# Low halves of the weights formed by GpSimd in pieces of 256 columns, in an fp32r four-layer transformer kernel

## The reference

```python
def conv_glu_ffn(n, w_up, conv_w, conv_b, w_down):
    gate, up = jnp.split(n @ w_up, 2, axis=-1)
    gp = jnp.pad(gate, ((0, 0), (CONV_WIDTH - 1, 0), (0, 0)))
    conv = conv_b
    for j in range(CONV_WIDTH):
        conv = conv + gp[:, j:j + s] * conv_w[j]
    return (jax.nn.silu(conv) * up) @ w_down
```

## Time and profile before

| what | value |
|---|---|
| median of 3 runs | 2933.06 us (2922.97 to 2939.97) |
| the profiled execution, its own time | 2924.7 us |
| its span, first to last instruction | 2922.2 us |
| granted TensorE clock, mean over the span | 0.957 |
| TensorE matmul busy | 2723.0 us, 93% |
| DVE busy | 1739.8 us, 60% |
| ACT busy | 1095.2 us, 37% |
| GpSimd busy | 1027.7 us, 35% |
| DMA engines, mean busy share | 21.6% |

### The profile page before, as it was taken

One profiled execution on the slowest core, in us unless ns is written; L12 is line 12 of the kernel. 1 busy time (PEld: TensorE's weight loads), 2 busy tenths in 40 slices (PEclk: granted clock), 3 DMA queues, 4 the chain that ended last, 5 costly groups with the idle time before them and its releaser, 6 DMA issues.

```text
span 2922.2 us, 34757 instructions
## 1 busy us (share of the span) xinstructions
PE 2723.0 (93%) x11434; PEld 2003.5 (69%) x11434; DVE 1739.8 (60%) x2256; ACT 1095.2 (37%) x1682; POOL 1027.7 (35%) x385
## 2 busy tenths in 40 slices
PE   6999999999998999999698988999989898899997
PEld 5654788887764678888375455788757644587875
DVE  4655774586386577377559346827634944583672
ACT  2345332223144343232543545323344345532333
POOL 2220344443321234444144123544424411344452
PEclk9998899999998899999799999999999998999999
DMA  3110123232211123222111011222311110122221
GB/s 135 65 44 30 65 93 104 90 102 86 79 51 36 43 86 107 87 96 98 39 58 51 29 37 65 96 91 93 103 66 58 44 43 22 63 92 96 94 97 68
DMA packets 56071, 212.17 MB, mean 73 GB/s; under 512 B 6193, under 2 KB 6449, under 8 KB 55857
## 3 DMA queue, kind: packets, MB, share of 16 engines
q1 hardware_dynamic: 55120, 209.60, 21.6%
q10 hardware_dynamic: 864, 1.44, 0.2%
HBM read 208.92 MB, written 2.10 MB: 72 GB/s over the span
## 4 chain that ended last, share of the span: by engine, by line
PE 72%; DVE 11%; ACT 6%; issue 5%; POOL 3%; DVEq 1%; DMA 0%; ACTq 0%; POOLq 0%
PE bank_G L464 20%; PE bank_G L466 19%; PE bank_G L465 19%; PE bank_S L1093 4%; POOL wlo L411 3%; PE bank_O L1103 2%; DVE conv_up L724 2%; PE bank_X L1113 2%; PE bank_S L511 1%; DVE mx L1985 1%; ACT whi L437 1%; DVE prod L744 1%; PE bank_X L1658 1%; PE bank_X L793 1%; DVE scores_t L1636 1%
## 5 line engine op out<-in xcount | busy, mean ns | idle before, releaser
L411 POOL TENSOR_TENSOR wlo<-raw,whi 128x1024 fp32r<-128x1024 f32 (+1 forms) x363 | 984.8, 2714 | 1760.7 <-ACT whi L437 1760.6
L464 PE MATMUL bank_G<-n_hi,whi 128*128 128x512 f32 x2392 | 977.4, 409 | 62.6 <-DVE n_lo L568 30.1
L466 PE MATMUL bank_G<-n_hi,wlo 128*128 128x512 f32 x2392 | 945.0, 395 | 0.0
L465 PE MATMUL bank_G<-n_lo,whi 128*128 128x512 f32 x2392 | 944.3, 395 | 0.0
L464 PEld LDWEIGHTS bank_G<-n_hi,whi 128*128 128x128 f32 x2392 | 458.1, 192 | 206.0 <-issue 69.5
L437 ACT ACTIVATE whi<-raw 128x1024 fp32r<-128x1024 f32 (+1 forms) x363 | 403.4, 1111 | 369.4 <-PE bank_G L466 353.8
L466 PEld LDWEIGHTS bank_G<-n_hi,wlo 128*128 128x128 f32 x2392 | 456.6, 191 | 99.5
L465 PEld LDWEIGHTS bank_G<-n_lo,whi 128*128 128x128 f32 x2392 | 458.2, 192 | 95.9 <-issue 7.7
L634 DVE SCALAR_TENSOR_TENSOR h<-h,mixed 128x512 f32 (+1 forms) x96 | 70.1, 730 | 393.3 <-ACT mixed L443 393.3
L464 PE MATMUL bank_G<-a_hi,whi 128*128 128x512 f32 x704 | 275.3, 391 | 5.6 <-DVE a_lo L746 3.6
L465 PE MATMUL bank_G<-a_lo,whi 128*128 128x512 f32 x704 | 274.0, 389 | 0.0
(11 more groups left out here) (280 smaller groups left out, 2706.3 us busy)
## 6 DMA issues: line engine op xcount, KB each, us to landing
raw<-in_w_mix_in SPq DMA_DIRECT2D x42, 512.0 KB, 3.2
raw<-in_w_out SPq DMA_DIRECT2D x32, 512.0 KB, 3.3
raw<-in_w_hyb_in SPq DMA_DIRECT2D x25, 512.0 KB, 3.3
raw<-in_w_diff_in SPq DMA_DIRECT2D x24, 512.0 KB, 3.3
raw<-in_w_up0a SPq DMA_DIRECT2D x22, 512.0 KB, 3.2
raw<-in_w_up0b SPq DMA_DIRECT2D x22, 512.0 KB, 3.2
raw<-in_w_up1a SPq DMA_DIRECT2D x22, 512.0 KB, 3.3
raw<-in_w_up1b SPq DMA_DIRECT2D x22, 512.0 KB, 3.3
```

What stands on the lines that cost most here:

```text
L411: pool.tensor_tensor(b.wlo[:, g.slot, 0:width], b.raw[:, g.slot, 0:width], b.whi[:, g.slot, 0:width], ALU.subtract).then_inc(b.lo_ready, 1)
L464: pe.matmul(out, b.whi[:, g.slot, w], hi[:, k, :], start=(k == 0), stop=False)
L465: pe.matmul(out, b.whi[:, g.slot, w], lo[:, k, :], start=False, stop=False)
L466: mm = pe.matmul(out, b.wlo[:, g.slot, w], hi[:, k, :], start=False, stop=(k == pieces - 1))
```

## The change

The subtraction of a tile is issued as several instructions of 256 columns each instead of one over the full width: four for a tile of 1024 columns, and six for one of 1408 (five of 256 and one of 128). Only the last of them raises lo_ready; the two waits ahead of the first stay. The product of the scan in mixer_pool is left as it was. The arithmetic, the buffers and the order of all other instructions are the same.

```diff
@@ constants
 ROW = 4 * T
 ARENA = 21056
+LO_PIECE = 256
 PAD = 2
@@ split_lo
     pool.wait_ge(b.hi_ready, g.at(1))
     wait(pool, b.gemm_done, g.at(-1))
-    pool.tensor_tensor(b.wlo[:, g.slot, 0:width], b.raw[:, g.slot, 0:width], b.whi[:, g.slot, 0:width],
-                       ALU.subtract).then_inc(b.lo_ready, 1)
+    for first in range(0, width, LO_PIECE):
+        x = slice(first, min(first + LO_PIECE, width))
+        ins = pool.tensor_tensor(b.wlo[:, g.slot, x], b.raw[:, g.slot, x], b.whi[:, g.slot, x], ALU.subtract)
+    ins.then_inc(b.lo_ready, 1)
```

## The result

| | kernel before | changed kernel |
|---|---|---|
| median of the runs | 2928.68 us (2922.97 to 2939.97, 7 runs) | 2949.21 us (2945.81 to 2950.34, 7 runs) |
| ratio to before, 95% interval | | 1.0058 [1.0039, 1.0077] |
| profiled execution, own time | 2924.7 us | 2950.11 us |
| its span | 2922.2 us | 2948.1 us |
| granted clock, mean | 0.957 | 0.956 |

The change makes the kernel slower by 0.58%. Between the two profiled spans lie 25.9 us, where the prediction's sum said 26; between the two medians lie 20.5. Lines behind the edit stand three higher now (L411 is L414, L464 is L467, L724 is L727).

The account below looks back on a forecast made before the run. TensorE was busy 93% of the span, with DVE held up by GpSimd and low halves sometimes awaited. Terms 3 + 12 + 5 + 4 + 3 + 7 - 4 - 4 = +26 on 2924.7, plus 8.4 to the median: 2959 us, range 2930 to 2990.

Parts of the forecast that it names:

- Block 1: Feed-forward up pairs of block 1: low half up to 1.47 us later just fits slack 1.5; +3 us for jitter.
- the first down tiles: First tile of each down group: in block 1 1.26 us late, four times, +5 us; in block 2 +4.
- Block 2, first failing term: Up pairs of block 2: low half 0.52 us late, 0.25 lost now regained; net 0.27 over 44 pairs, +12 us.
- two tiles behind each other don't add up: Up pairs of block 2: two late tiles cost no double, since a late tile gives the next its time back.
- The loss of now: Up pairs of block 2: TensorE already loses 0.25 us a pair through DVE's chain; it goes, as prod comes sooner.
- few other starts: Third tiles of some groups: an estimated four starts wait for GpSimd, 0.39 to 0.84 us each, +3 us.
- The mixers: Mixers of block 2: some four starts in each wait for a later low half, half absorbed; 8 x 0.9, +7 us.
- DVE hogs the port: Rival: dense DVE taps in 18 mixer turns keep GpSimd out at piece boundaries; +36 to +72 us on top, chance 0.09.
- The norms and the attention: Gains from DVE held up less: -4 us at three norm places, -4 us in attention.
- DVE freed: Rival: fewer DVE instructions slip in, block 2's slack of 0.77 us holds; -26 us, 2907 us, chance 0.14.
- The pieces flow without a gap: Rival: DVE is not let in between pieces and is held longer; +24 us, within the 0.55 for late low halves.
- No difference: Rival for the whole kernel: both effects stay below 10 us or cancel; 2933 us, chance 0.22.

Follow-up runs that it names:

- e9: e6 with DVE waiting for the up tile's low half ahead of its third tap; 2947.17 us, ratio 1.0055 to the kernel before.
- e5: Kernel before with only the gate tiles of block 2's up groups in pieces of 256 columns; 2941.78 us, ratio 1.0051.
- e11: The changed kernel with one DVE wait for a low half in each mixer of block 2; 2936.13 us, ratio 1.0028 to the kernel before.
- the last version: e10 with one DVE wait for a low half in each mixer of block 2; 2899.89 us, ratio 0.9897 to the kernel before.
- e10: Kernel before with piece sizes chosen per group (256, 512 or whole), first down tiles of block 2 whole; 2907.52 us, ratio 0.9926.
- e4: The changed kernel with pieces of 128 columns everywhere instead of 256; 3023.16 us, ratio 1.0324 to the kernel before.
- e6: Kernel before with only the up tiles of block 2's up groups in pieces of 256 columns; 2952.94 us, ratio 1.0082.
- e3: The changed kernel with pieces of 512 columns everywhere instead of 256; 2919.09 us, ratio 0.9962 to the kernel before.

## Why the prediction was right, and where its terms were not

The forecast was 2959 us, within 2930 to 2990, slower. The median is 2949. The 10 us between are nearly all the offset: I added 8.4 us to the profiled execution, because the three runs shown had a median of 2933.06, and seven runs have one of 2928.68; the changed kernel's median lies 0.9 below its own profiled execution.

**The prices held.** 0.13 us a piece and 0.45 for each DVE instruction let in, both taken from whole low halves, measure 0.14 (256 columns at 2.16 ns are 0.55, the spacing with DVE idle is 0.69 to 0.70 in some 580 boundaries) and 0.45 (1.14 to 1.15 in some 330 more; e9 shows the same by taking it away). TensorE's 0.13 us behind a low half, which the prediction took from a row that it did not show, is the same in every pair of the changed kernel (1843.75 to 1843.88). The row, of the kernel before:

```profile
1803.28 2.83 POOL L411 TENSOR_TENSOR wlo<-raw,whi 128x1024 fp32r<-128x1024 f32 x1 [3.62 <-ACT whi L437]
```

The estimates from the Trainium skill's figures were 0.06 us a piece (GPSIMD Engine Reference, Performance versus the Vector engine) and 0.17 (Performance pitfalls for Q7 kernels); the trace's 0.14 lies between them, nearer the second.

**Block 1** came out as worked: the low halves take 3.72 to 3.81 us, at most 1.42 more than before against the 1.47 that I had, which fits the slack of 1.5; +2.1 against +3 in the pairs, and the first down tiles 1.23 us late against 1.26.

**Block 2, first failing term: 0.27 a pair.** The low half was 0.60 late and not 0.52, and TensorE lost another 0.14 because it starts worse after a stall (below). And "two tiles behind each other don't add up" was right as a result and wrong as a reason. There are two loops of different length, and the up tile's became the longer one. The loss of now, 0.25 a pair, did go away, but that was in the gate loop. Had the gate tile alone been cut, the working would have given 12.0 us (e5's expectation did), and 11.57 was measured: the step "a late low half costs a pair its lateness" holds in a loop of one pair and is halved in a loop of two.

**The "few other starts", second failing term: +3 against +16.9.** Of the 16.9, 4.05 only hand back gains booked elsewhere, and 5.1 are the clock of these executions, as said above. What is left, some 8 us, still is more than twice the term. I had counted four starts. The out groups were not in the count at all: DVE's h, sq and acc stand ready at each boundary there, so that in block 1 all their tiles went from 5.44 to 5.61 us. And behind a long idle time of GpSimd two tiles follow each other without slack. At the third tile of out1 TensorE waited 2.12 us before and 3.34 after, and then lost 2.7 us more by the granted clock, 0.65 instead of 1.00 over that tile. The sum had no term for what a wait does to the clock. Timeline of the changed kernel (the row of GpSimd holds that tile's four pieces and the first two of the next):

```profile
988.00 6.26 POOL L414 TENSOR_TENSOR wlo<-raw,whi 128x256 fp32r<-128x256 f32 x6 [70.63 <-ACT whi L440]
...
992.57 0.79 PE L467 MATMUL bank_G<-n_hi,whi 128*128 128x512 f32 x1 [3.34 <-POOL wlo L414]
```

**The mixers, third: +7 against 0.** The turns gained more by the freed DVE than I allowed, 3.3 and 5.3 us up to the 16th tile (the second in part because the stage ahead of that tile lasted 16.54 us in this execution of the kernel before, and 11.43 in its first mixer), and the rival "DVE hogs the port" took it back. I had priced that rival at 18 turns with 2 to 4 us each. It was real in two places at 6.1 us each, of which the stage behind takes 0.8 off, hidden in the sum until e11 showed it: without it the change would cost 0.28% and not 0.58. So a mechanism that I had given 0.09 made up some 11 us of the net loss, 0.3 percentage points by the medians, beside the one that I had named.

**Gains outside the sum.** The second tile of each down group comes 0.35 us sooner behind the first in block 1 and 1.0 in block 2, eight groups, -5.4 with small ones, since DVE's part of it is freed; the first one of block 2 loses nothing, as the pair ahead of it already stalls. The norms and the attention gained 11.5 against 8.

So that the sum was right to 0.1 us was luck, by compensation: the pairs of block 2 and the other starts cost 6.8 and 13.9 us more than I said, and the down groups (5.4 and 4), the mixers (6.9), the norms (1.9), the attention (1.6) and block 1 with its first down tiles (1.0) came out that much lower. Measured by the medians it was 5 us too high. What was right as such is the sign and its two mechanisms: the low half of block 2 comes late in every pair, and DVE's gain is worth little there.

**The rivals.** "DVE freed" falls: two instructions get in, not one. "The pieces flow without a gap" falls: DVE is let in at some 330 boundaries. The Trainium skill (GPSIMD Engine Reference, Instruction dispatch) has each core start the next instruction once its share of the last is done; what I read into that, that nothing gets in between, the trace does not bear out. "No difference" is excluded by the interval.

## What to carry to other kernels

Where two engines exclude each other by whole instructions, cutting one engine's long instruction into pieces gives the other time and makes the cut work longer, by one waiting instruction per boundary: cut only where the cut work has that much slack, tile by tile, and then as coarsely as frees the other (here two pieces, in one tile of each pair). Look for loops over several rounds before pricing a late step: in a loop of two rounds the lateness counts half, and a second, shorter loop may have room for it. And look for long runs of one engine without any wait: one wait placed in the run was worth 7.6 of the 26 us that the last version gains. And before booking a gain, look whether the next start hangs on another chain: the first norm's gain went into a longer wait two tiles later.

## What the runs showed of the hardware

- *A dense run of DVE can keep a GpSimd instruction out until it is over*: 16.52 us for 256 columns, 17.55 for 512 in e10. The Trainium skill (SBUF — State Buffer, Who interferes with whom) has the side that issues first hold the ports for a whole instruction. The single hand-overs in the pairs agree with it, as the third tap that waits from 1840.32 to 1840.77. The long ones do not: 23 taps that were issued after the piece at 1575.02 went ahead of it.
- *What decides that isn't shown.* It is not the overlap of the taps alone. GpSimd instructions that follow each other directly get in at each boundary in the middle of overlapping taps (1550.70). Those that come after an idle time got in where at most four taps of the run had started, and with six or more they stood until the run ended or reached the wait, except in e4: there pieces of 128 columns came in at the sixth tap and, in the same run, at the eighteenth, and got in at once. GpSimd and DVE in the first mixer of block 2 in e4:

```profile
1614.35 6.56 POOL L414 TENSOR_TENSOR wlo<-raw,whi 128x128 fp32r<-128x128 f32 x8 [3.69 <-ACT whi L440]
...
1610.27 22.10 DVE L1988 SCALAR_TENSOR_TENSOR mx<-cpad,vec,mx 128x512 f32<-128x512 f32 x28
```

- *TensorE restarts slowly after a short stall, at the full granted clock too.* Its first matmul lasts 0.49 us instead of 0.39, and the first six take 1.50 us instead of 1.36 (1847.71 to 1849.21 in e6, against 1840.32 to 1841.68 without a stall): 0.14 us each time, in 44 pairs 6 us.
- *The clock can fall behind a wait.* Behind 3.34 us of waiting 24 matmuls took 8.28 us at a granted clock of 0.65, behind 2.12 us at the same place 5.57 at 1.00. The length of the wait alone does not decide it: in e3 TensorE waited 2.07 us there, and the tile took 7.19.
- *The granted clock of the same code differs between executions*: 0.87 and 0.79 in one stretch of 60 us, two times 6.2 us in one execution.
